# First layer and output projections: evicting a block ahead of a weight split on VectorE

## The reference, cut to what matters

```python
def mla_stick_breaking_mixer(u, w_in, g_cq, w_uq, g_ckv, w_ukv, w_out):
    proj = u @ w_in                      # c_q, c_kv, k_r, q_b, k_b, v_b
    ...
    q_a = rms_norm(c_q, g_cq) @ w_uq     # 8 heads: 64 plain + 32 rotary columns
    q_a = concat(q_a[..., :64], apply_rope(q_a[..., 64:], cos, sin))
    kv = rms_norm(c_kv, g_ckv) @ w_ukv   # 8 heads: 64 key + 64 value columns
    ...
    # group A (8 heads): softmax attention over chunks that are allowed
    # group B (8 heads): stick-breaking attention
    z = einsum(q_b, k_b) * scale_b
    log_keep = where(before, log_sigmoid(-z), 0)
    log_between = cumsum(log_keep, reverse=True) - log_keep
    w_b = where(before, exp(log_sigmoid(z) + log_between), 0)
    ...
    return concat([o_a, o_b]) @ w_out

h = h + mixer(rms_norm(h, g_mix), ...)   # out0, and out1 to out3 in the later layers
h = h + mlp(rms_norm(h, g_ffn), ...)     # gu0/dn0, gu1/dn1, up2/dn2, up3/dn3
```

## Time and profile before

| | |
|---|---|
| median of 3 runs | 1264.97 us (1262.21 to 1265.29) |
| the profiled execution's own time | 1263.89 us |
| its span | 1262.1 us |
| TensorE busy | 1237.3 us, 98% |
| VectorE busy | 883.7 us, 70% |
| ScalarE busy | 768.1 us, 61% |
| GpSimd busy | 447.8 us, 35% |

### The profile page before, as it was taken

One profiled execution on the slowest core, in us unless ns is written; L12 is line 12 of the kernel. 1 busy time (PEld: TensorE's weight loads), 2 busy tenths in 40 slices (PEclk: granted clock), 3 DMA queues, 4 the chain that ended last, 5 costly groups with the idle time before them and its releaser, 6 DMA issues.

```text
span 1262.1 us, 25272 instructions
## 1 busy us (share of the span) xinstructions
PE 1237.3 (98%) x8594; PEld 1122.2 (89%) x8594; DVE 883.7 (70%) x1557; ACT 768.1 (61%) x1486; POOL 447.8 (35%) x413
## 2 busy tenths in 40 slices
PE   6999999999999999999999899999999999999998
PEld 6988888888988988888889599999999889888887
DVE  5687877877577677778799975555447766877654
ACT  6476777765555587776566854444446776655433
POOL 2011477731000167761133037760001220688200
PEclk9999999999999999999999999999999999999999
DMA  7642566666665456657555055555556443666665
GB/s 264 183 126 84 184 194 188 184 219 205 218 184 159 135 184 192 188 182 232 169 167 154 22 163 184 169 183 182 170 165 195 153 131 102 185 190 190 203 194 154
DMA packets 65760, 218.65 MB, mean 173 GB/s; under 512 B 9152, under 2 KB 13456, under 8 KB 65552
## 3 DMA queue, kind: packets, MB, share of 16 engines
q1 hardware_dynamic: 63344, 210.99, 54.6%
q10 hardware_dynamic: 2336, 6.58, 1.6%
HBM read 214.04 MB, written 1.08 MB: 170 GB/s over the span
## 4 chain that ended last, share of the span: by engine, by line
PE 73%; issue 8%; DVE 7%; POOL 6%; ACT 4%; DMA 1%; POOLq 0%; ACTq 0%; SPq 0%; DVEq 0%
PE bank L376 19%; PE bank L360 12%; PE bank L362 11%; PE bank L361 11%; PE bank L377 10%; POOL scratch L659 3%; DVE wlo L344 2%; DVE uhi_ulo L442 1%; POOL ahi_alo L663 1%; POOL scratch L661 1%; PE bank L1033 1%; ACT whi L339 1%; ACT prob L1071 1%; PE bank L1018 1%; DVE scratch L651 1%
## 5 line engine op out<-in xcount | busy, mean ns | idle before, releaser
L344 DVE TENSOR_TENSOR wlo<-raw,whi 128x1024 fp32r<-128x1024 f32 (+1 forms) x391 | 502.8, 1297 | 162.3 <-ACT whi L339 161.0
L339 ACT ACTIVATE whi<-raw 128x1024 fp32r<-128x1024 f32 (+1 forms) x391 | 407.6, 1047 | 178.2 <-PE bank L377 93.5
L376 PE MATMUL bank<-uhi_ulo,whi 128*128 128x512 f32 x960 | 336.5, 394 | 0.8 <-DVE uhi_ulo L442 0.7
L377 PE MATMUL bank<-uhi_ulo,wlo 128*128 128x256 f32 x960 | 269.2, 280 | 0.0
L360 PE MATMUL bank<-uhi_ulo,whi 128*128 128x272 f32 (+1 forms) x816 | 241.9, 296 | 10.4 <-DVE wlo L344 10.1
L362 PE MATMUL bank<-uhi_ulo,wlo 128*128 128x272 f32 (+1 forms) x816 | 234.5, 287 | 0.0
L361 PE MATMUL bank<-uhi_ulo,whi 128*128 128x272 f32 (+1 forms) x816 | 233.6, 286 | 0.0
L376 PEld LDWEIGHTS bank<-uhi_ulo,whi 128*128 128x128 f32 x960 | 180.2, 188 | 42.5 <-DVE uhi_ulo L442 1.7
L376 PE MATMUL bank<-ahi_alo,whi 128*128 128x512 f32 x608 | 212.4, 393 | 0.0
L377 PEld LDWEIGHTS bank<-uhi_ulo,wlo 128*128 128x128 f32 x960 | 180.4, 188 | 0.1
L360 PEld LDWEIGHTS bank<-uhi_ulo,whi 128*128 128x128 f32 x816 | 154.8, 190 | 17.9 <-issue 16.5
(11 more groups left out here) (307 smaller groups left out, 1817.8 us busy)
## 6 DMA issues: line engine op xcount, KB each, us to landing
raw<-stream SPq DMA_DIRECT2D x391, 512.0 KB, 4.0
scratch<-decay ACTq DMA_DIRECT2D x8, 416.0 KB, 3.5
scratch<-relh ACTq DMA_DIRECT2D x8, 384.0 KB, 3.5
scratch<-scratch SPq DMA_DIRECT2D x60, 34.0 KB, 2.7
constants<-consts SPq DMA_DIRECT2D x1, 1300.0 KB, 10.6
h<-xT SPq DMA_DIRECT2D x4, 256.0 KB, 5.1
out<-h SPq DMA_DIRECT2D x8, 128.0 KB, 3.9
scratch<-scratch SPq DMA_DIRECT2D x16, 16.0 KB, 3.1
```

Source lines behind the costliest of these rows:

```text
L339: act.activation(whi[:, s, 0:w], raw[:, s, 0:w], ACT.Copy).then_inc(w_hi, 1)
L344: dve.tensor_tensor(wlo[:, s, 0:w], raw[:, s, 0:w], whi[:, s, 0:w].bitcast(F32), ALU.subtract).then_inc(w_lo, 1)
L376: pe.matmul(dst, hi, both[:, :, c0 + i, FIRST], start=first and i == 0, stop=end, skip_group_check=True)
L377: mm = pe.matmul(dst[:, 0:SEQ], lo, both[:, 0, c0 + i, FIRST], start=False, stop=end, skip_group_check=True)
```

## The change

In pairs s = 0 and s = 3, the second latent block of the pair (m1, m7) is evicted without a split before it; its split comes after the masking of the second half. In the output projections, block 6's split moves from before the low half of chunk 5 to after the eviction of block 6. On TensorE, chunk 5 of block 3 of out0 moves behind chunk 3 of blocks 0 to 2. SyncE, ScalarE and GpSimd are unchanged.

```diff
@@ resid_dve
                 late = per == 1 and m == DC - 1 and gname is not None
+                behind = per == 1 and m == DC - 2 and gname is not None
                 for u in range(per):
-                    if m >= ahead and not late:
+                    if m >= ahead and not late and not behind:
                         split_lo(dve, At(START[name] + m * per + u + AHEAD))
...
                 dve.tensor_tensor(h[:, m, cols], src[:, 0:width(cols)], h[:, m, cols],
                                   ALU.add).then_inc(evac, 1)
+                if behind:
+                    split_lo(dve, At(START[name] + m + AHEAD))
@@ mix_pe
-            part(3, (0, 1, 4, 5), first=True)
+            part(3, (0, 1, 4), first=True)
             for j in range(3):
                 part(j, (3,), last=True)
-            part(3, (6, 2, 7, 3), last=True)
+            part(3, (5, 6, 2, 7, 3), last=True)
@@ mix_dve
-            def unit(kind, i):
+            def unit(kind, i, late=False):
                 n = MIX_AT[kind, i]
                 j = n - START["mix"]
-                split_lo(dve, *mix_ahead(j))
+                if not late:
+                    split_lo(dve, *mix_ahead(j))
...
-                unit("m", 2 * s + 1)
+                late = s in (0, 3)
+                unit("m", 2 * s + 1, late)
                 stick_split_dve(dve, s, 1)
+                if late:
+                    split_lo(dve, *mix_ahead(MIX_AT["m", 2 * s + 1] - START["mix"]))
```

## The result

The changed kernel takes 1269.57 us (median of 5 runs, 1269.18 to 1271.10), the kernel before 1264.97 (5 runs, 1262.21 to 1265.29). The ratio is 1.0042, with a 95% interval of 1.0031 to 1.0052: slower by 5.3 us (3.9 to 6.6) by the ratio, by 4.6 us by the two medians. The forecast was 1268.2. For a time slower by over 0.3%, which is what came, the prediction had 33%, behind 63% for a smaller difference.

The account below looks back on a forecast made before the run. TensorE, busy for 98% of the span, was taken as the bound. Terms +2.20 + 2.0 - 0.35 - 0.45 - 0.1 = +3.3 us, stated as +3.2, gave 1268.2 us from the median 1264.97; range 1263.0 to 1270.8.

Parts of the forecast that it names:

- First pair, +2.2: Pair s = 0: the swap waits for the late split, moving the second rotation from 61.72 to 63.92, +2.20 us.
- Last pair, +2.0: Pair s = 3: second rotation moves from 111.47 to 113.77, value matmuls start +2.0 us later, removed 1.05 us wait included.
- The signs that were named for it: Swaps start near 60.2 and 110.1; VectorE idles near 3 us; TensorE waits over 2 us before the last scores.
- Chunk, -0.35: Moved chunk 5 of block 3 in out0: the gap of 0.42 us at 125.57 nearly closes, -0.35 us.
- Seventh block, -0.45 in out0 and -0.1 in the others: Output projections: last two low halves come about 0.5 us earlier, -0.45 us in out0, -0.1 us in the others.
- The sum: Whole kernel: +2.20 + 2.0 - 0.35 - 0.45 - 0.1 = +3.3 us, stated as +3.2.
- The fifth gap: TensorE's wait of 0.24 us for VectorE at 88.64, third pair, read as both engines running in step.
- The landing: SyncE's queue: the swap cannot land ahead of its load, so the full 2.2 us are paid each time.
- (a), swap off the path: The rotation does not move; first pair gives at most 0.1 us, last 0.3 us: 1263.7 us in all; 12%.
- (b), clock drop: Last pair: an idle stretch of 2.3 us takes TensorE to half speed, up to 1.5 us, 1269.7 us; 15%.
- (c), half absorbed: One swap lands sooner, or VectorE catches up in pairs two and three: +1.5 us, 1266.5 us; 13%.

Follow-up runs that it names:

- the version with the swap first: The changed kernel, with SyncE starting the swaps of m1 and m7 ahead of the load: 1263.39 us, ratio 0.9992.
- the first pair alone: The kernel before with only the split in pair s = 0 moved: 1267.11 us, ratio 1.0018.
- the kernel with the moved splits alone: The kernel before with only the splits in pairs s = 0 and s = 3 moved: 1268.95 us, ratio 1.0030.
- the last pair alone: The kernel before with only the split in pair s = 3 moved: 1266.04 us, ratio 1.0016.
- the last two versions: The kernel before with all eight swaps ahead of their loads, 1264.57 us; the same with the pairs' moved splits and the moved chunk, 1262.63 us.

## Why the prediction was right or wrong

**First pair, +2.2: right.** The sums came 0.45 us earlier (0.46 forecast). In the time of the kernel before (less 1.23 us), the second rotation starts at 65.11 - 1.23 = 63.88 (63.92 forecast), the scores are 0.93 us late and the next queries 2.12. Nothing behind it took that back.

**Last pair, +2.0: right in what delays it and in the total, wrong in where TensorE waits.** VectorE enters the pair 1.46 us late. With that taken off, the first split's end, which the load follows at once, moves by 112.39 - 1.23 - 107.39 - 1.46 = 2.31 us (2.30 forecast) and the rotation by 116.44 - 1.23 - 111.47 - 1.46 = 2.28. At the values it is 3.35 - 1.40 = 1.95 us in the changed kernel. The signs that were named for it split. The swaps start where forecast (61.43 - 1.23 = 60.20, and 110.13 with the carried delay of 1.46 taken off), VectorE idles 2.57 and 2.50 us at L1747, the first pair's scores wait 1.20 us. But TensorE does not wait over 2 us before the last pair's scores: it waits 1.68 us one chunk earlier, for L973 behind the rotation. And it still waits 0.97 us at L1528 (L1531 in the changed kernel). The prediction had it about 0.5 us ahead there; the kernel before shows why that could not be:
```profile
107.06 0.85 ACT L954 ACTIVATE probT<-bank 128x384 f32<-128x384 f32 x2
...
107.61 0.42 DVE L1737 TENSOR_TENSOR scratch<-bank,rstd 128x256 f32<-128x256 f32 x1
```
The probability copy ends at 107.91, the eviction at 108.03. Without the eviction only 0.12 us of the 1.05 could go, however early the swap comes; that is why the version with the swap first gained next to nothing in this pair.

**Chunk, -0.35: right** (-0.36).

**Seventh block, -0.45 in out0 and -0.1 in the others: wrong, and this is the step that failed.** It cost 0.22 us in out0 and 0.54 in out1 to out3 together. The step saw that the low half of block 5 would be clear of GpSimd's addition and dropped the other side: the split and the low half of block 6 move beside the next two additions. The statement "the last two low halves come about 0.5 us earlier" had to be a sum over all four VectorE operations, and that sum is +0.22. The wait for ScalarE of 0.58 us moved from block 6 to block 5, as the step had it. That the waits of out1 and out3 were small did bound a gain; it says nothing on a loss.

**The sum.** By the trace: 2.12 - 0.57 (pair 2) - 0.15 + 1.95 - 0.36 + 0.22 + 0.86 (behind out0) = 4.07 us, against +3.3. Of the 0.86, 0.54 is the out projections; the other 0.3 are steps at 641 and near 1011 to 1024 us of a kind that kernels without any part of the change there show too. So the out projections were off by +1.3 and the pairs by -0.85, of which 0.55 to 0.6 is the slow swap in the profile of before. Two errors thus partly cancel in this sum, and that is luck. Against an execution of before without that swap the change would cost about 4.6 us, inside the interval of 3.9 to 6.6; the two medians differ by 4.6 too, 1.4 more than the 3.2 forecast, which is nearly what the out projections were off by. The ratios of the parts sum to 0.30% + 0.06% - 0.05% = 0.31%, against 0.42% for the whole, with intervals of 0.1% either way on each. The fifth gap, from which the prediction read that VectorE and TensorE run in step, belongs to the slow swap and does not show that; that the delay is carried is shown by the first pair alone.

**The landing.** The prediction argued that the swap cannot land ahead of its load. Of each swap's two transfers the first did, by 0.11 to 0.86 us in all eight swaps of before; the second, for which the second rotation waits, landed 0.34 to 0.41 us behind the load in all eight. So the argument holds for the transfer that matters.

**The rivals.** (a), swap off the path: refuted, by rotations 2.3 us late. Putting the swap first is what takes it off the path. That kernel's 1263.39 is near the 1263.7 of (a), but by luck: (a) counted 0.55 us won in the out projections and 0.3 in the last pair, where the traces have 0.77 lost and about 0.1 won, and the kernel before itself ran 0.7 us faster beside this experiment than in the first runs. (b), clock drop: true of some executions. It is shown in the last pair once, in the kernel with the moved splits alone, at 1.2 us where 1.5 was allowed for, and not in the profile of the changed kernel. The mean granted clock over runs is 0.9966 for the changed kernel and 0.9964 for the moved splits alone, against 0.9972 for the kernel before and 0.9979 with the swap first, so it may add to the median; how often it strikes was not counted. (c), half absorbed: no, apart from the slow swap of before.

## What to carry to other kernels

An instruction that signals other engines is more than its own time: before a split is moved, follow its semaphore into the queues that wait for it, and look at what stands behind that wait. A small transfer on the critical path goes ahead of the bulk load in the queue, not behind it. And when two steps on one engine swap places, add up all of them beside the neighbour engine's work, not only the one that gets faster. A wait counts as removable only down to the next thing that it would wait for, and a difference of under 1 us between two single profiles is looked for in a third before it is explained.

## What the runs showed of the hardware

In the kernel before, a 16 KB swap transfer issued behind a 512 KB load on the same queue lands after 2.4 to 3.7 us (median 3.1), with the swaps ahead of their loads after 1.7 to 2.4 (median 2.0). A load that went out shortly before lengthens it, whichever block that load belongs to: in the kernel with all swaps first a transfer took 1.7 to 2.0 us where the load before had landed, and 2.2 to 2.4 where one had gone out 1.3 to 2.0 us before; in the last pair of the version with moved splits, moved chunk and all swaps first, where the load of the block before had gone out 0.7 and 1.3 us earlier, the two took 3.1 and 3.2.

TensorE's clock fell in some executions of a stretch and not in others, and where it matters it costs 1.5 us. At about 641 us TensorE waits for GpSimd in all twelve profiles. Windows of the kernel with the first pair alone there, in which it waits 1.91 us:
```profile
638.00:642.00 4.00, 3.06 (x25) 2.84 (x23) 3.48 (x5) 1.65 (x3) 1.79 (x3) 1.00 0.76 224
642.00:646.00 4.00, 3.04 (x16) 1.54 (x17) 4.00 (x6) 0.85 (x4) 2.40 (x3) 0.68 0.62 180
```
and of the kernel with the last pair alone, with a wait of 1.50 us:
```profile
638.00:642.00 4.00, 3.23 (x26) 3.01 (x24) 4.00 (x7) 1.85 (x3) 2.04 (x3) 1.00 0.55 151
642.00:646.00 4.00, 3.27 (x26) 2.48 (x27) 4.00 (x6) 1.67 (x6) 2.41 (x3) 1.00 0.83 236
```
Over the next 5 us the shift of the first goes from +1.95 to +3.47, that of the second stays at +1.55. The clock fell behind the seven waits of 1.82 to 2.10 us and not behind the five of 1.50 to 1.81. But the length of the wait alone does not decide: in the last pair it fell behind 1.69 us in the kernel with the moved splits alone and not behind 2.05 us in the one with the last pair alone. What decides is open.

A fallen clock can also cost nothing. In the stretch of the earlier trace rows the kernel before had 0.63; windows of the kernel with the last pair alone (mean clock of the whole trace 1.00), where TensorE is idle for over half of the first 4 us:
```profile
696.00:700.00 4.00, 1.87 (x18) 1.30 (x19) 3.93 (x18) 3.81 (x19) 1.21 (x2) 1.00 0.00 0
700.00:704.00 4.00, 2.68 (x24) 1.58 (x21) 3.83 (x22) 4.00 (x18) 0.75 (x2) 1.00 0.00 0
```
and of the kernel before with the swaps first:
```profile
696.00:700.00 4.00, 2.25 (x16) 1.48 (x18) 3.94 (x19) 3.90 (x18) 1.95 (x3) 0.80 0.00 0
700.00:704.00 4.00, 4.00 (x23) 3.05 (x21) 3.86 (x21) 3.70 (x15) 0.00 (x0) 0.50 0.00 0
```
With its full clock the first gained nothing on the kernel before (shift +1.55 on either side), so the fall of the earlier trace rows, from which rival (b) took its price, cost nothing; the second lost 1.24 us against it.

Falls of the clock go with the slow end of the times: of the 35 runs of the kernel before beside the single pairs and the last two versions, the eight with a mean clock of 0.996 or less took 1265.81 to 1267.25 us, the other 27 took 1262.36 to 1265.53. The fall at 641 us is also why the last rows of the table above are no measure of a part.
